# Prompt rows loaded feature-major, and the sample's last iteration rebuilt, in a hybrid decoder step on one core

## The reference, cut to what is computed

```
h   = rmsnorm(x) * (1 + scale_m) + shift_m          # scale, shift, gate from silu(c) @ w_ada + b_ada
u   = h @ w_in                                      # columns: a | b | q | k | v | g, 512 each
glu = a * sigmoid(b)
conv = silu(layernorm(depthwise conv of glu, 31 taps))      # sample: the 30 earlier inputs are state_conv
q, k = rotary(q), rotary(k)                         # 4 heads of 128
o   = decayed causal retention of q, k, v           # sample: the state is state_ret, S (128x128 per head)
ret = groupnorm(o) * silu(g)
x   = x + gate_m * ([conv, ret] @ w_out)
h2  = rmsnorm(x) * (1 + scale_f) + shift_f
scores = sigmoid(h2 @ w_router); top 6 of 64 experts (4 of 8 groups)
x   = x + gate_f * (shared expert(h2) + sum of weighted experts(h2))
y   = rmsnorm(x)                                    # new convolution and retention states too
```

## Time and profile before

| what | value |
|---|---|
| median of 3 runs | 1590.01 us (1589.70 to 1591.05) |
| the profiled execution, its own time | 1590.49 us |
| its span in the trace | 1588.7 us |
| mean granted clock of TensorE | 0.958 |
| TensorE busy | 1444.5 us, 91% |
| VectorE busy | 845.3 us, 53% |
| GpSimd busy | 494.7 us, 31% |
| ScalarE busy | 213.0 us, 13% |
| moved by DMA | 370 MB, mean 233 GB/s |

### The profile page before, as it was taken

One profiled execution on the slowest core, in us unless ns is written; L12 is line 12 of the kernel. 1 busy time (PEld: TensorE's weight loads), 2 busy tenths in 40 slices (PEclk: granted clock), 3 DMA queues, 4 the chain that ended last, 5 costly groups with the idle time before them and its releaser, 6 DMA issues.

```text
span 1588.7 us, 17546 instructions
## 1 busy us (share of the span) xinstructions
PE 1444.5 (91%) x5851; PEld 653.0 (41%) x5851; DVE 845.3 (53%) x2135; ACT 213.0 (13%) x358; POOL 494.7 (31%) x426
## 2 busy tenths in 40 slices
PE   4899999999999999988799998999979999999947
PEld 2344454555545455554343332344423333333313
DVE  1147778998988999575533323333333232333317
ACT  1111231312222231222000000000000000000003
POOL 0001010121211111304545444454544545454410
PEclk9999999999999999958799999999999999999978
DMA  9987211211120000603399999999999999999975
GB/s 333 329 316 266 96 43 67 82 40 70 40 83 27 32 29 27 189 33 114 119 369 326 344 370 360 364 373 364 373 366 358 375 363 374 353 368 360 372 219 239
DMA packets 93690, 370.17 MB, mean 233 GB/s; under 512 B 17763, under 2 KB 29447, under 8 KB 68461
## 3 DMA queue, kind: packets, MB, share of 16 engines
q1 hardware_dynamic: 69637, 304.77, 49.5%
q0 software_dynamic: 23968, 64.35, 16.2%
HBM read 323.09 MB, written 62.62 MB: 243 GB/s over the span
## 4 chain that ended last, share of the span: by engine, by line
DMA 37%; PE 30%; DVE 19%; issue 7%; SPq 4%; ACT 2%; POOL 1%; POOLq 0%; DVEq 0%; ACTq 0%
DMA acc_rows<-W,kT 17%; DMA acc_rows<-xr,kT 15%; PE U L649 9%; PE R L702 8%; DVE cv L1188 7%; PE U L831 5%; PE R L847 2%; SPq L396 2%; DMA W<-in_w_ada 2%; DMA acc_rows<-xr,shared_f 1%; DMA W<-h_rows,q_r 1%; PE R L613 1%; SPq L403 1%; PE U L673 1%; PE U L757 1%
## 5 line engine op out<-in xcount | busy, mean ns | idle before, releaser
L649 PE MATMUL U<-W,hT 128*128 128x512 f32 x864 | 386.2, 601 | 1.2 <-issue 1.2
L1188 DVE SCALAR_TENSOR_TENSOR cv<-win,cw,cv 128x128 f32<-128x128 f32 x960 | 254.8, 344 | 1.4
L831 PE MATMUL U<-W,cat 128*32 128x512 f32 (+2 forms) x1072 | 239.0, 614 | 5.8 <-issue 3.7
L831 PE MATMUL U<-W,hT 128*32 128x512 f32 (+2 forms) x976 | 237.9, 608 | 6.0 <-issue 6.0
L847 PE MATMUL R<-W,glu 128*32 128x512 f32 (+2 forms) x1024 | 240.8, 597 | 1.3 <-DVE glu L1458 1.3
L649 PEld LDWEIGHTS U<-W,hT 128*128 128x128 f32 x864 | 162.5, 193 | 189.0 <-issue 189.0
L1445 DVE STREAM_TRANSPOSE cat<-W 128x1024 f32<-128x1024 f32 x33 | 67.4, 2042 | 203.0 <-DMA W<-h_rows,q_r 200.1
L1445 DVE STREAM_TRANSPOSE hT<-x_t 128x1024 f32<-128x1024 f32 x33 | 67.3, 2039 | 189.5 <-DMA x_t<-h_rows,q_r 168.0
L847 PEld LDWEIGHTS R<-W,glu 128*32 128x32 f32 (+2 forms) x1024 | 84.1, 138 | 150.8 <-issue 149.3
L831 PEld LDWEIGHTS U<-W,hT 128*32 128x32 f32 (+2 forms) x976 | 88.5, 144 | 131.2 <-issue 129.7
L831 PEld LDWEIGHTS U<-W,cat 128*32 128x32 f32 (+2 forms) x1072 | 85.4, 139 | 135.1 <-issue 130.9
(11 more groups left out here) (252 smaller groups left out, 1189.9 us busy)
## 6 DMA issues: line engine op xcount, KB each, us to landing
W<-in_w SPq DMA_DIRECT2D x192, 1024.0 KB, 17.6
W<-in_w_ada SPq DMA_DIRECT2D x24, 1024.0 KB, 8.7
W<-in_w_in SPq DMA_DIRECT2D x6, 2048.0 KB, 19.9
W<-acc_rows SPq DMA_DIRECT2D x16, 512.0 KB, 9.5
x_rows<-xr SPq DMA_DIRECT2D x9, 512.0 KB, 3.3
h_rows<-xr SPq DMA_DIRECT2D x9, 512.0 KB, 2.7
x_t<-in_x_prompt SPq DMA_DIRECT2D x8, 512.0 KB
W<-in_w_out SPq DMA_DIRECT2D x1, 4096.0 KB, 17.4
```

The lines of the kernel that those rows point to most:

```text
L649: last = mm(U[BANK[g]][:, :], hT[:, k, :], w_in[:, k, 512 * g:512 * g + 512], start=k == 0, stop=k == KT - 1)
L831: last = mm(U[1][cols, :], xgT[z][:, k, cols], w13[:, :, k, :], start=k == 0, stop=k == KT - 1)
L1188: ins = v.scalar_tensor_tensor(cv[:, c, :], win[:, c, w:w + P], cw[:, c, w:w + 1], cv[:, c, :], ALU.mult, ALU.add)
```

## The change

The change has three parts.

First, the prompt. The host lays the prompt rows out a second time, by feature (`x_prompt_t`, per tile 128 features by 8 groups by 128 rows). SyncE loads a tile of it straight into hT, the operand of the projections, once the last projection has read the tile before (`load_turned`). The rows themselves are still loaded for the sum of squares. TensorE spreads the reciprocal root of each row over all partitions with one product into X (`spread_std`, in place of x_trans), VectorE multiplies hT by it (`scale_turned`), and ScalarE applies scale and shift as one column each in eight operations (`hT_scale`). VectorE no longer scales x_t and GpSimd no longer adds the shift, except for the sample, whose rows are transposed as before. The order of TensorE in an iteration changes: q_r's transposes, positions, k_r's transposes, mix_out, and only then projections GB and GA.

Second, the sample. Its tail and route leave the common body and get code for 8 rows: products and norms over 8 rows or columns where they had 128 (mix_out's accumulators are 8 rows by 512), the convolution state loaded in the layout in which it is used (`state_conv_t`) instead of being transposed, the masks of v_t and the update of the states on ScalarE instead of VectorE, with the old state added by a second product with the identity in TensorE (`state_product`). mix_out of tile 7 goes behind the cross products; the up products of blocks 0 and 1, the positions and top_k of the last tiles change places; on GpSimd the gathers 0 to 3 and the list writes change places.

Third, AHEAD is 4 instead of 5: the first routed block is block 4, and its gather is issued behind scatter 1, when the second part of the slot lists is known.

The diff, cut to what is spoken of:

```diff
-AHEAD = 5
+AHEAD = 4
...
+            sp.dma_start(hT[:, :, :], t["x_prompt_t"][0:P].rearrange("p (k n) -> p k n", k=KT)).then_inc(xT_in, 16)
...
-                sp.wait_ge(x_posed, i + 1)
+                sp.wait_ge(norm1_ssq, i + 1)
...
+            def load_turned(i):
+                sp.wait_ge(uk_done, i + 1)
+                sp.dma_start(hT[:, :, :], t["x_prompt_t"][bass.ds((i + 1) * P, P)].rearrange("p (k n) -> p k n", k=KT)).then_inc(xT_in, 16)
...
-            for p in range(8, 19):
+            for p in range(8, 15):
+                load_ada(p)
+            load_turned(0)
...
+            load_turned(1)
...
+                load_turned(i)
...
+            sp.dma_start(sconv, t["state_conv_t"]).then_inc(sconv_in, 16)
...
+            def spread_std(i):
+                pe.wait_ge(h_scaled, i + 1)
+                pe.wait_ge(h2T_ready, floor(i - 2))
+                mm(X[:, 0:P], rstd1.to_broadcast([P, P]), ident[:, :], start=True, stop=True).then_inc(x_posed, 1)
...
+                at = slice(512 * (n % 2), 512 * (n % 2) + 512)
+                mm(R[:, at], k_s[:, P * h:P * h + P], vmask[:, 2 * half:2 * half + 2, :, P * h:P * h + P], start=True, stop=False)
+                mm(R[:, at], ident[:, :], S0[:, 2 * half:2 * half + 2, :, h, :], start=False, stop=True).then_inc(state_mm, 1)
...
             def body(i, front=True, tail=True, route=True, nxt=True, place=True):
                 j, m = i - 1, i - 2
-                prompt = not (isinstance(j, int) and j == TP)
                 if tail:
                     four(q_r, q_posed, win_ready, j + 1, q_rot, j + 1)
+                if place:
+                    positions(m - 2, pick, i - 1)
+                if tail:
+                    four(k_r, k_posed, qT_ready, j + 1, k_rot, j + 1)
+                if route:
+                    mix_out(m)
                 if front:
                     pe.wait_ge(hT_ready, i + 1)
                     project(i, GB, ub_done, sg_ready, i)
-                if place:
-                    positions(m - 2, pick, i - 1)
-                if route:
-                    mix_out(m)
-                if tail:
-                    four(k_r, k_posed, qT_ready, j + 1, k_rot, j + 1)
                 if front:
                     project(i, GA, ua_done, k_rot, i)
...
-                if nxt:
-                    x_trans(i + 1)
+                if nxt and isinstance(i, int) and i + 1 == TP:
+                    x_trans(TP)
+                elif nxt:
...
+            positions(TP - 3, pick, TP)
...
+            few_rows(q_r, T4, q_posed)
...
+            for h in range(H):
+                for b in range(NS):
+                    last = mm(U[0][:, h * NS + b:h * NS + b + 1], S0[:, b // 2, b % 2, h, :], qT[:, h, b:b + 1], start=True, stop=True)
+            last.then_inc(s_cross_done, 1)
...
+            few_sum(cv, sum1_done)
+            mix_out(TP - 1)
...
+            few_sum(sq, sum2_done)
...
+            few_rows(o_t[:, :, :].rearrange("p h e -> p (h e)"), R24, ret_posed)
...
+            for n in range(2):
+                for k in range(KT):
+                    last = mm(U[n][0:NS, :], cat_s[:, k, :], w_out[:, k, 512 * n:512 * n + 512], start=k == 0, stop=k == KT - 1)
+            last.then_inc(wout_done, 1)
...
+            rows2_trans(TP - 1, hT_ready, NT)
...
+            state_product(0)
+            state_product(1)
+            router(TP - 1, TP)
+            state_product(2)
+            state_product(3)
+            pe.wait_ge(score_ready, TP)
             positions(TP - 2, pick, NT)
-            mix_out(TP)
...
+            up(0, shw_all, 0)
...
+            for n in range(H, 2 * H):
+                state_product(n)
...
-            up(0, shw_all, 0)
-            rows2_trans(TP, hT_ready, NT)
-            hidden_trans(0)
-            pe.wait_ge(dest_ready, TP)
-            router(TP, TP)
-            up(1, shw_all, 1)
+            positions(TP - 1, pick, NT)
             down(0, shw_all)
             positions(TP, pick_s[:, :], NT)
             hidden_trans(1)
...
+            def hT_scale(i):
+                act.wait_ge(h_ready, i + 1)
+                act.wait_ge(ab_ready, 2)
+                for k in range(KT):
+                    last = nc.scalar.activation(hT[:, k, :], hT[:, k, :], ACT.Identity, scale=A_col[:, k:k + 1], bias=B_col[:, k:k + 1])
+                last.then_inc(hT_ready, 1)
...
+            act.wait_ge(k_rot, NT)
+            act.wait_ge(ret_done, TP)
+            for h in range(H):
+                cols = slice(HD * h, HD * h + HD)
+                nc.scalar.activation(k_s[:, cols], k_r[0:NS, cols], ACT.Copy, scale=1.0 / GAMMA[h])
+            for b in range(NS):
+                last = nc.scalar.activation(vmask[:, b // 2, b % 2, :], v_t[0:NS, :], ACT.Copy, scale=ident[0:NS, b:b + 1])
+            last.then_inc(vmask_ready, 1)
+            act.wait_ge(s_cross_done, 1)
...
+            def state_update(n):
+                h, half = n // 2, n % 2
+                act.wait_ge(state_mm, n + 1)
+                nc.scalar.activation(S0[:, 2 * half:2 * half + 2, :, h, :], R[:, 512 * (n % 2):512 * (n % 2) + 512].rearrange(
+                    "p (k c e) -> p k c e", k=2, c=2), ACT.Copy, scale=float(GAMMA[h])).then_inc(state_upd, 1)
+            state_update(0)
+            state_update(1)
+            score(TP - 1)
+            state_update(2)
+            state_update(3)
...
-                v.scalar_tensor_tensor(x_t[:, :], x_t[:, :], rstd1, A_m, ALU.mult, ALU.mult).then_inc(h_scaled, 1)
...
+                    v.reciprocal(rstd1, std1).then_inc(h_scaled, 1)
...
+            def scale_turned(i):
+                dve.wait_ge(x_posed, i + 1)
+                dve.wait_ge(xT_in, 16 * (i + 1))
+                v.tensor_tensor(hT[:, :, :], hT[:, :, :], X[:, 0:P].unsqueeze(1).to_broadcast([P, KT, P]), ALU.mult).then_inc(h_ready, 1)
...
+            def sample_tail():
+                place(TP - 3, pick, TP)
...
+                for c in range(CT):
+                    link(v.tensor_tensor(cprod, cbuf[:, c], cw[:, c, :].unsqueeze(1).to_broadcast([P, NS, CW]), ALU.mult))
+                    link(v.tensor_reduce(cv[:, c, 0:NS], cprod, AX.X, ALU.add))
+                    ins = v.tensor_scalar(cv[:, c, 0:NS], cv[:, c, 0:NS], cvec[:, c:c + 1], None, ALU.add)
+                    if c < CT - 1:
+                        link(ins)
+                ins.then_inc(conv_ready, 1)
...
-            xpose(0)
-            residual(TP)
-            norm2(TP)
-            place(TP - 1, pick, NT)
...
+            sample_tail()
+            residual(TP - 1)
+            norm2(TP - 1)
+            top_k(TP - 2)
+            sample_residual()
+            place(TP - 2, pick, NT)
+            sample_norm2()
+            top_k(TP - 1)
             blk_hid(0)
             blk_hidT(0)
             dve.wait_ge(router_done, NT)
             xpose(1)
+            place(TP - 1, pick, NT)
             top_k(TP)
             place(TP, pick_s[:, :], NT)
...
+            gather(0)
...
             fill_list(TP - 3)
-            gather(0)
             ret_out(TP)
+            gather(1)
             fill_list(TP - 2)
-            gather(1)
+            fill_list(TP - 1)
             gather(2)
-            fill_list(TP - 1)
+            fill_list(TP, NS)
             gather(3)
-            fill_list(TP, NS)
...
             scatter(0)
-            gather(4)
             scatter(1)
             pool.wait_ge(slot_ready, 2)
+            gather(4)
...
+    taps = np.pad(arrays["state_conv"][0], ((0, 0), (0, 1), (0, 0))).reshape(NS, CW, CT, P)
+    arrays["state_conv_t"] = np.ascontiguousarray(taps.transpose(3, 2, 0, 1).reshape(P, CT * NS * CW))
+    turned = arrays["x_prompt"][0].reshape(TP, P, KT, P)
+    arrays["x_prompt_t"] = np.ascontiguousarray(turned.transpose(0, 3, 2, 1).reshape(SEQ, D))
...
```

361 lines of the change are left out of this document (200 added, 161 removed).

## The result

The changed kernel takes 1604.05 us (1602.92 to 1608.57), against 1589.86 us for the kernel before in the same runs: a ratio of 1.0097, 95% interval 1.0081 to 1.0112. Measured again later beside other kernels it took 1603.42 against 1590.09, ratio 1.0089 (1.0068 to 1.0109). I had forecast 1585.3 with a range of 1574 to 1597. The sign was wrong and the time lies outside the range.

What follows compares the result with a forecast made beforehand. It took VectorE's chain to bound the loop, latency the tail and DMA bytes the expert stretch. From 1590.49, start and loop +1.3, tail -6.5 and experts +0.5 gave 1585.8, against the median 1585.3; range 1574 to 1597.

Steps and rivals of the forecast that it cites:

- The start: Iteration 0: the first feature-major load of 0.5 MB stands in the queue ahead of the weights, +1.4 us.
- Iteration 1: No mix_out covers hT there, so copies and eight ScalarE operations delay projection GB and idle time costs clock: +6.2 us.
- Iterations 2 and 3: Mixer loop without place: VectorE is 2.8 us earlier and TensorE's wait on cv is gone, -3.8 us together.
- Iterations 4 to 7: Mixer loop: the wait on cv stays and VectorE is the bound, four times -0.4 us, -1.6 us.
- Iteration 8: Last loop iteration: its operand still comes by transposes, but VectorE starts it unhindered, -0.9 us.
- The tail: Last projection of iteration 8 to first expert weight load: a latency chain of 119.8 us instead of 126.35, -6.5 us.
- The expert stretch: From first expert weight load to end: block 4 ends when block 5 did, bytes set the end, +0.5 us.
- Rival 2: Expert stretch: the scatter chain, not the bytes, sets it; late first scatter and late block 4 carried through, +6, 1591; chance 0.15.
- Rival 3: Loop: VectorE waits for a feature-major load landing 2 us later, +11.8 us, 1597; chance 0.20 including worse.
- Rival 4: Loop: TensorE waits for the feature-major load; held excluded up to 7 us by mix_out, no chance given.
- The signs that I had named: Wrong if VectorE waits over 2 us for xT_in, tail over 124 us, or DMA share after 860 under 0.98.
- The rule on table loads: Tail: the skill's 2.66 us per ScalarE table switch would add 4.1 us, leaving a gain of 2.4; forecast rejected it.

Runs made afterwards that it cites:

- Experiment 10: Kernel of experiment 8 with ScalarE doing the second norm's square and root ahead of GB's sigmoid in iterations 2 and 3: 1584.07 us, ratio 0.9966.
- experiment 4: Changed kernel with, in iteration 1 alone, hT scaled ahead of the qT and kT copies and k_r transposed behind projection GB: 1597.91 us, ratio 1.0052.
- experiment 1: Changed kernel with the prompt part undone, sample part and AHEAD 4 kept: 1592.93 us, ratio 1.0023.
- experiment 2: Changed kernel with AHEAD 5 and gather 4 behind scatter 0 again: 1594.75 us, ratio 1.0031.
- experiment 5: The changed kernel itself, unaltered, run again beside other kernels: 1603.42 us, ratio 1.0089.
- experiment 6: Changed kernel with the prompt part undone and AHEAD 5, so the sample part alone: 1588.17 us, ratio 0.9990.
- Experiment 9: Changed kernel with prompt part undone, AHEAD 5, gathers 2 and 3 early, plus the last four state products behind positions(7): 1581.50 us, ratio 0.9943.
- experiment 11: Changed kernel with tiles 2 to 7 feature-major, root first, AHEAD 5, gathers early and state products late: 1578.69 us, ratio 0.9928.
- experiment 8: Changed kernel with AHEAD 5, gathers 2 and 3 early, and the prompt part only from tile 2 on: 1583.91 us, ratio 0.9961.
- experiment 12: Changed kernel with AHEAD 5 and gathers 2 and 3 early, prompt part whole: 1591.94 us, ratio 1.0011.

## Why the prediction was wrong, by its own steps

**The start** (+1.4) measured +1.2 in this pair of traces, and that closeness is luck: the start ends at 101.3 to 102.8 in six executions with the feature-major load of tile 0 and at 98.3 to 102.4 in eight without it (means 102.1 and 99.8).

**Iteration 1** (+6.2, upper bound +8) measured +9.2. The chain of copies and eight operations was right to 0.6 us. From the end of GK, the last projection of iteration 0, the copies took 8.1 us (I had 7.9) and the eight operations 3.19 instead of 3.9. Each takes 478 to 493 ns, like the row that I took, but they overlap, since nothing waits between them: they start 0.39 us apart. So projection GB came 4.4 us later within the iteration, not 5.0. The loss of clock in it was 2.0 to 2.7, not 1.7. In two of the five executions with this iteration 1 that is all, and it comes to +6.8. In the other three, this trace among them, the rest of the iteration is 1.9 to 2.8 us longer. That is the term that I had put at nothing: I had let the idle time end with the projection, and did not ask whose loads are issued behind it and what TensorE's clock does at the waits for them. The table of iteration 1 shows low clock there in all three and a longer last wait in two. What sets it off is open.

**Iterations 2 and 3** (-3.8) measured -1.5. The step "the wait is gone" failed. VectorE was early as computed, but mix_out now stands ahead of GB. The sigmoid of GB comes so much later on ScalarE, and the root of the second norm is queued behind it. I had followed the moved projection on TensorE and not in the queue of the engine that evacuates it. Experiment 10 shows it for 1.2 of the missing 2.3 us; with the root out of the way VectorE waits for projection GA itself. The last 1.1 us are not taken apart.

**Iterations 4 to 7** (-1.6) measured +1.5. VectorE is the bound there, as forecast, and where the clock holds an iteration takes 69.0 instead of 69.6, a little better than my -0.4. What I had left out is the clock: with the changed loop one to three iterations lose 1.6 to 2 us each, and which ones differs between executions (the table). The kernel before has such a loss too, mostly in iterations 5 and 6; iteration 6 is the longest in all fourteen executions (71.9 to 74.9), and why is open. The sum of iterations 4 to 8 is 352.0 to 353.9 in five executions with the old operand and 353.3 to 357.1 in nine with the new one. What makes the clock fall in one execution and not in another is open.

**Iteration 8** (-0.9): +1.7 in the changed kernel, where mix_out runs at low clock, +0.1 in experiment 4, where it doesn't (69.67; I had 68.7). So the gain that I saw in VectorE's free start was none, and the clock took the rest.

**The tail** (-6.5, bounds -2 to -14) measured -1.9, and -5.6 to +0.2 in the other executions with the same order of the tail (experiments 1, 2, 4, 5, 6). The chain was the right one: positions(7), six list writes, gather 2, its transpose, the line. Up to the end of mix_out of tile 7 it agrees to 0.5 us (33.5 after iteration 8, forecast 33). The sample's mix_out took 16.50, I had 15.5. The eight state products take 2.11 us each; the steps of my chain left 1.6 to 1.75 for each. By the end of the sample's router this is 84.1 against 78.4, and positions(7) starts at 99.6 against 94.5. The step that was mis-sized is thus the state products, with the clock of the sample's mix_out beside it. Experiment 9 shows that they count in full up to positions(7) and for three quarters up to the first load, but only for a quarter between experiments 10 and 11. The tail varies by 6 us between executions of one order, so the -1.9 of this one says little by itself.

**The expert stretch** (+0.5, bounds -3 and +7) measured +7.5, with the final sums. I had named the parts: gather 4 lands 34 us after the first load (36.2), TensorE idles 10 us (10.78), scatter 0 is 7 us behind (7.4). The step that failed is "block 4 ends when block 5 did", and with it the refill 2 us earlier. Block 4 started 2.5 us later than block 5 had, and its up product took 2.6 more at low clock, so the refill came 5.1 later and the DMA engines ran dry. The queues being full before and after does not help: what is missed in a gap is not made up. The bytes do set this end. Rival 2 had two parts: a late first scatter carried through the chain is refuted by experiment 2 (747.3 us with scatter 0 still 7.4 behind the first load); the late block 4 did cost, but by the gap in the transfers.

**Rival 3** (the load lands late) did not happen: the page gives 3.5 us from issue to landing for the eight loads. That of iteration 2 took 4.2, and VectorE waited 2.13 us for it; in iterations 3, 4, 5 and 7 it waited 1.3 to 1.5. Rival 4 was rightly excluded in the loop; in iteration 1, without mix_out, it is the largest loss of the change.

**The signs that I had named** all came: the 2.13 us of VectorE in iteration 2, the tail of 124.4 us, and a DMA share of 0.88 from 851.92 to 871.92 (1.03 in the 28 us behind it). The first is worth 0.7 us in one iteration and was no cause of the loss; the tail and the share point at the two steps above.

**The rule on table loads.** On ScalarE, a table load of iteration 3 right behind other work, and the operation that follows:

```profile
269.86 0.19 ACT L1027 ACTIVATION_READ_ACCUMULATOR rt<-xr 128x1 f32 x1
270.06 1.28 ACT L1029 ACT_TABLE_LOAD   x1
271.36 0.29 ACT L1029 ACTIVATE st<-st,eps_c 128x1 f32<-128x1 f32 x1
```

The load starts 0.01 us behind the operation before it, takes 1.28, and the root follows after 0.02 us. The Trainium skill, "ScalarE: Activation LUTs", What ACT_TABLE_LOAD costs, adds a drain for 2.66 us a switch; this trace does not agree, and no part of the lost time is such a drain. That the tail gained 1.9, near the 2.4 that this rule gave, is coincidence: its loss stands on TensorE, at the state products.

In the chances, 0.20 for rival 3 and worse was the only place for a time above 1597, and it was given to the wrong mechanism. Six of the seven terms came out above the forecast: I had followed each saving on the engine that made it, and not the wait that it left on the next one.

## What to carry to other kernels

When an instruction is moved behind another, follow it in three queues: its own, that of the engine which evacuates its result and everything queued behind that evacuation, and the DMA queue whose buffers it frees. A prefetch is worth what covers it in each iteration, so look for the iteration that has no cover (the first) and keep the old way there (experiment 8 against 12: 8.0 us). In a stretch that is bound by bytes, look for the moment at which the transfers run dry, not only for its ends; here a gather that had to pass a landing scatter brought it about. And before a loss is explained from one trace, read the same stretch in the traces of the experiments that don't touch it.

## What the runs showed of the hardware that I had not expected

- An activation of 128x128 with a column each for scale and bias took 478 to 493 ns, but eight of them took 3.19 us together, so they start 0.39 us apart. Four with Silu, 492 ns each and with a wait between one and the next, took 2.07 us, 0.53 apart.
- A scatter of 0.5 MB took 12.2 us to land while twelve loads of 1 MB were in flight (799.29 in the changed kernel), and 11.5 in the kernel before, also behind twelve loads; the next one, issued at 812.41, waited 11.48 us for it.
- TensorE idle for 4 us at 105 left the next projection at 9.06 us instead of 7.03 (granted clock 1.00 from 100 to 105, 0.62 and 0.69 in the two stretches of 5 us behind), and at 9.49 to 9.69 in four other executions; idle times of 2 to 2.5 us in the loop did so in some executions and not in others, at the same place of the same program.
